# Order of the moving columns in the wide fp32r matmuls of a three-block network on one Trainium2 core

## What is computed

```python
def macaron_half_ffn(x, pre_g, post_g, w_gate, w_up, w_down):   # 1024 -> 2816 -> 1024
    h = rmsnorm(x, pre_g)
    h = (jax.nn.silu(h @ w_gate) * (h @ w_up)) @ w_down
    return x + 0.5 * rmsnorm(h, post_g)
...
def reference(x, ...):
    x = first_block(x, ...)    # ffn, sparse attention + short convolution, ffn; ffn, RWKV, ffn
    x = second_block(x, ...)   # ffn, SSD + attention, attention over a memory, ffn
    return third_block(x, ...) # 16 meta tokens ahead: ffn, gated linear attention, ffn; ffn, windowed attention, ffn
```

## Time and profile before

| | |
|---|---|
| three executions | 3,265.66, 3,267.18, 3,271.96 us; median 3,267.18 |
| the profiled execution | span 3,253.4 us from first to last instruction; the median lies 13.8 us above it |
| mean granted TensorE clock | 0.977 of full speed |
| PE, PEld (weight loads) | busy 96% and 92% of the span, 27,478 instructions each |
| DVE, ACT, POOL | busy 55%, 47%, 28% |
| HBM | 479 MB read, 148 GB/s over the span |

### The profile page before, as it was taken

The page is one execution under the profiler, slowest core; times in us unless marked ns, Lnnn a source line. Parts: engine busy times, 40 slices in busy tenths (PEclk is TensorE's granted clock), DMA queues, the critical chain, the costliest instruction groups (busy, mean ns, idle before and its releaser), DMA issues.

```text
span 3253.4 us, 64299 instructions
## 1 busy us (share of the span) xinstructions
PE 3111.1 (96%) x27478; PEld 2988.1 (92%) x27478; DVE 1803.0 (55%) x3040; ACT 1523.1 (47%) x2564; POOL 907.7 (28%) x481
## 2 busy tenths in 40 slices
PE   8999999999899999998999999999989999998999
PEld 8998899998688999998898889999979999997898
DVE  5456555647765645447567544454543546556554
ACT  5444454543422544437656444444333544544453
POOL 3321132331333232322221213222213332332232
PEclk9999999999999999999999999999989999998999
DMA  6542355564201555553343435535423454552354
GB/s 241 194 167 87 117 195 169 196 194 161 91 3 34 185 193 175 184 184 122 125 156 110 137 133 195 189 134 177 136 91 104 169 176 145 192 182 71 113 193 136
DMA packets 133388, 484.55 MB, mean 149 GB/s; under 512 B 14959, under 2 KB 17151, under 8 KB 132399
## 3 DMA queue, kind: packets, MB, share of 16 engines
q1 hardware_dynamic: 131120, 470.25, 43.1%
q0 software_dynamic: 1984, 10.19, 1.0%
HBM read 479.34 MB, written 1.05 MB: 148 GB/s over the span
## 4 chain that ended last, share of the span: by engine, by line
PE 82%; DVE 10%; ACT 5%; issue 2%; POOL 1%; DMA 0%; DVEq 0%; SPq 0%; ACTq 0%; POOLq 0%
PE ps L185 81%; DVE lo L162 2%; ACT hi L182 1%; ACT arena L182 1%; DVE tmp L170 1%; PE ps L193 1%; DVE sq L162 1%; DVE arena L170 1%; ACT L182 1%; DVE yT L170 1%; DVE arena L162 1%; POOL small L162 1%; POOL lo L162 0%; DVE small L179 0%; DVE xT L162 0%
## 5 line engine op out<-in xcount | busy, mean ns | idle before, releaser
L162 POOL TENSOR_TENSOR lo<-raw,hi 128x1024 fp32r<-128x1024 f32 x271 | 689.7, 2545 | 1683.3 <-ACT hi L182 1683.3
L182 ACT ACTIVATE hi<-raw 128x1024 fp32r<-128x1024 f32 x814 | 854.0, 1053 | 419.7 <-PE ps L185 312.2
L185 PE MATMUL ps<-hh,lo 128*128 128x256 f32 x3696 | 1019.5, 279 | 0.0
L162 DVE TENSOR_TENSOR lo<-raw,hi 128x1024 fp32r<-128x1024 f32 x543 | 703.7, 1299 | 513.6 <-ACT hi L182 493.4
L185 PE MATMUL ps<-hh,hi 128*128 128x256 f32 x3456 | 961.9, 281 | 24.3 <-ACT arena L182 8.8
L185 PE MATMUL ps<-hl,hi 128*128 128x256 f32 x3456 | 928.0, 279 | 1.2 <-DVE hl L162 1.2
L185 PEld LDWEIGHTS ps<-hh,lo 128*128 128x128 f32 x3696 | 702.6, 190 | 0.0
L185 PEld LDWEIGHTS ps<-hh,hi 128*128 128x128 f32 x3456 | 658.1, 190 | 32.8 <-ACT arena L182 12.2
L185 PEld LDWEIGHTS ps<-hl,hi 128*128 128x128 f32 x3456 | 641.6, 190 | 1.6 <-DVE hl L162 1.4
L185 PE MATMUL ps<-hfh,lo 128*128 128x256 f32 (+1 forms) x1760 | 489.5, 278 | 0.0
L185 PE MATMUL ps<-hfh,hi 128*128 128x256 f32 (+1 forms) x1520 | 422.7, 278 | 0.0
(11 more groups left out here) (385 smaller groups left out, 4716.6 us busy)
## 6 DMA issues: line engine op xcount, KB each, us to landing
raw<-in_l_ffn_w_gate SPq DMA_DIRECT2D x88, 512.0 KB, 3.3
raw<-in_l_ffn_w_up SPq DMA_DIRECT2D x88, 512.0 KB, 3.4
raw<-in_l_ffn_w_down SPq DMA_DIRECT2D x88, 512.0 KB, 3.6
raw<-in_g SPq DMA_DIRECT2D x88, 512.0 KB, 3.3
raw<-in_u SPq DMA_DIRECT2D x88, 512.0 KB, 3.3
raw<-in_d SPq DMA_DIRECT2D x88, 512.0 KB, 3.3
raw<-in_ffn_w_gate SPq DMA_DIRECT2D x44, 512.0 KB, 3.4
raw<-in_ffn_w_up SPq DMA_DIRECT2D x44, 512.0 KB, 3.5
```

Of the source, the lines that this page charges most:

```text
L162: return self.e.tensor_tensor(o, a, b, op)
L182: return self.e.activation(o, a, f, **kw)
L185: return self.e.matmul(o, a, b, start=first, stop=final, skip_group_check=loose)
```

## The change

The moving operand and the output of every matmul that goes through `mm3`, and of the two opening loops (`Ffn.firsts`, `Mixer.first`), get another order of columns where their number is a multiple of 256. The view `p (i a c) -> p a i c` with i = 2 and c = 4 takes columns 0 to 3 of the first half, 0 to 3 of the second half, 4 to 7 of the first, 4 to 7 of the second, and so on. Operand and output have the same order, so each result column is written to the place that it had. 272 columns are no multiple of 256 and stay as they were. The instructions, their order, waits and addresses of buffers are the same on all engines.

```diff
     def mm(self, o, a, b, first=True, final=True, loose=False):
         return self.e.matmul(o, a, b, start=first, stop=final, skip_group_check=loose)
 
+    def mw(self, o, a, b, first=True, final=True, loose=False):
+        return self.mm(halves(o), a, halves(b), first, final, loose)
+
     def mm3(self, o, a, b, first=True, final=True, loose=False):
-        self.mm(o, a[0], b[0], first, False, loose)
-        self.mm(o, a[0], b[1], False, False, loose)
-        return self.mm(o, a[1], b[0], False, final, loose)
+        self.mw(o, a[0], b[0], first, False, loose)
+        self.mw(o, a[0], b[1], False, False, loose)
+        return self.mw(o, a[1], b[0], False, final, loose)
...
+def halves(ap):
+
+
+    if ap.shape[-1] % 256:
+        return ap
+    return ap.rearrange("p (i a c) -> p a i c", i=2, c=4)
...
@@ Ffn.firsts
-                pe.mm(bank[:, 0:T], hi, K.X[T][0][:, k, 0:T], k == 0, False)
-                pe.mm(bank[:, 0:T], lo, K.X[T][0][:, k, 0:T], False, False)
+                pe.mw(bank[:, 0:T], hi, K.X[T][0][:, k, 0:T], k == 0, False)
+                pe.mw(bank[:, 0:T], lo, K.X[T][0][:, k, 0:T], False, False)
             pe.wait_ge(*self.entry.hl(k))
             for i, bank in enumerate(banks):
-                t = pe.mm(bank[:, 0:T], K.W.col(u + i, k)[0], K.X[T][1][:, k, 0:T], False, k == 7)
+                t = pe.mw(bank[:, 0:T], K.W.col(u + i, k)[0], K.X[T][1][:, k, 0:T], False, k == 7)
...
@@ Mixer.first
-                    pe.mm(bank[:, 0:T], w, src[0][:, k, 0:T], k == j == 0, False)
+                    pe.mw(bank[:, 0:T], w, src[0][:, k, 0:T], k == j == 0, False)
...
-                t = pe.mm(bank[:, 0:T], W.col(u + i, k)[0], src[1][:, k, 0:T], False, k == 7)
+                t = pe.mw(bank[:, 0:T], W.col(u + i, k)[0], src[1][:, k, 0:T], False, k == 7)
```

## The result

The changed kernel takes 3,455.3 us (median of 4 runs, 3,448.1 to 3,463.0) against 3,266.4 us for the kernel before beside it (3,256.4 to 3,272.0): a ratio of 1.058, 95% interval 1.054 to 1.062. It is slower by 5.8%, and lies above the end of my range.

A forecast was written before the change was run, and what follows sets the result against it. The prediction took TensorE's matmul spacing as the bound; savings of 27.8, 6.9 and 5.2 us, less a microsecond, gave 39 us off 3,267.2, so 3,228 us. The range was 3,188 to 3,340 us.

The forecast's parts named there:

- What bounds the kernel: Whole kernel: time is the number of wide matmuls times their spacing on TensorE, 113.3 ns, with TensorE 96% busy.
- What the spacing is made of: Wide fp32r matmuls: 6.6 ns over the array's time and the slower pace come from moving columns and next weights colliding.
- the second state: 256-column fp32r matmuls: same shapes and address remainders also run at 117.8 ns instead of 113.3; 1,098 intervals counted.
- the deeper gain: Rival for the 256-column matmuls: fp32r reaches the transposes' 110 ns or a little below, saving 66 us, 3,201 us; chance 0.18.
- The price of the new order: Split-order matmuls: shown by no row, so bounded; nearest taken as 111.5 ns, the pace of non-transposed 128-column fp32 rows.
- the sum: Changed 256- and 512-column matmuls: 27.8, 6.9 and 5.2 us saved, less a microsecond, gives 39 us.
- Half clock: About 300 matmuls at half clock gain nothing, taking a microsecond off the saving.
- No change: Rival for the whole kernel: time stays within 0.2% (6.5 us); chance 0.12.
- The slower rival: Every 256-column matmul pays the 117.8 ns pace, 73 us more, 3,340 us; chance 0.26, of it 0.10 beyond 3,340.

The follow-up runs named there:

- m3: Separate kernel without the network: blocks of 72 fp32r matmuls, one weight column repeated, many widths; 256 columns 113 and 118 ns in one piece, 126 split at 512 bytes.
- m1: Separate kernel without the network: blocks of 144 fp32r matmuls, varying split side, group size and weights; 114.1 ns in one piece, 127.2 with both split.
- m4: Separate kernel without the network: blocks of matmuls with weights cut to 4 and 16 columns, bf16 and plain fp32 added; one piece fp32r 114.7 ns, bf16 109.2.
- m2: Separate kernel without the network: blocks of 72 fp32r matmuls, halves further apart or groups at fixed steps; 127.6 ns at 512 bytes, 121.1 at 576, 134.5 stepping by 80.
- a2: Changed kernel with only the output in split order, moving operand read in one piece; 3,270.1 us, ratio 0.9995 to the kernel before.

## Why the prediction was wrong, point by point

- *What bounds the kernel* was right: TensorE's spacing, nothing else. The loss came through it, waits on converted weights stayed in single microseconds (4.7 and 3.7 us in total, for VectorE's and GpSimd's), and 272 columns and the other engines stayed as they were.
- *What the spacing is made of* is the step that failed. I put the 6.6 ns over the array's time, and the second state, down to the moving columns of one matmul and the weights of the next getting in each other's way. That was my estimate, and no run shows it. Rows 6 seemed to show that without this (2.51 - 0.28) / 20 = 111.5 ns, or the transposes' (1.04 - 0.27) / 7 = 110, are enough. But those rows are plain fp32, which takes (3.61 - 0.38) / 15 = 215.3 ns over 256 columns where fp32r takes 113.3; they show a read with slack, and the right comparison, a full-pace read without weights, was not in the trace of before. Measured, it is 113.3 ns with 4 weight columns: there was nothing to win but the second state's few us. I had seen that not one fp32r interval lay under 113 ns, and gave it too little weight against the deeper gain and none against the forecast.
- *The price of the new order*: taken 111.5, bounded above by 117.8, measured 126.7. No run shows the sum's 111.5 for 256 columns of fp32r, the least is 113.3. Nor does one show its 215.3 for 512 columns, which is plain fp32's spacing over 256: fp32r took 228 there before, 252 after, and 233 in one piece in the blocks. The 111.5 was no price of a read at all: fp32r with 128 or 192 moving columns takes 112.0 to 112.5 too (L35 and L39 of m3). The upper bound was the price of the second state, not of an unknown read pattern. The slowest row of that matmul, the half-clock one at 214, lay above what came, and I left it out of the range.
- *Half clock.* I took about 300 matmuls for it; the trace has 173. It is a microsecond of the sum and changes nothing.
- *No change* was nearer than my forecast as to the gain: one piece takes 114.1 ns with 128 weight columns (L34 of m1) and 114.7 with 4 (L32 of m4), so that less of the weights wins nothing. They aren't wholly without effect, though: their place moves the spacing of one piece by up to 6 ns (120.8 at L47 against 114.6 at L63 of m2).
- *The slower rival* had the sign, and the wrong price: the spacing is the same in gate, up and down products, but at 126.7 ns above 118, which I had set down as the mark that the jumps themselves cost. A time beyond 3,340 us by such a cost had a chance of 0.10 in the text, and came. Even this wasn't the whole: what a jump costs depends on where it leads and on the operand's type.
- *At the output* I gave the broken order no price of its own; it was worth nothing here (a2, ratio 0.9995).

## What to carry to other kernels

A fp32r moving operand at full clock should be read in one piece, or in runs of 256 bytes at least (free in the network, ratio 0.997; one kernel of blocks, m3, had 118.9 ns for such runs, the value of the second state). Of the finer orders tried here, those of bf16 and of plain fp32 in 16-byte groups were free (109.2 and 215.9 ns, as in one piece), and the one on the PSUM side (ratio 0.9995). Before a collision is put down as the reason of an excess, look for a row in which one of the two parties is missing while the other keeps its full pace; a row in which both run slower proves nothing. And ask of a row that gives a price whether something else sets it, as here, probably, the least time of a pair of weight load and matmul (112 ns). Where no row shows a new access pattern, the upper bound is the slowest row of that instruction, however far it lies.

## What the runs showed of the hardware that I had not expected

- fp32r doesn't reach the pace of bf16: 113.3 ns (or 117.8) for 256 columns and 233 for 512, where bf16 takes 109.2 and 215.8 with a weight load before each too.
- 256 columns are favoured: 272 take 123.3 to 126.7, 10 ns or more for 16 columns more. Fewer gain little: 128, 192 and 240 take 112.0, 112.5 and 113 with 128 weight columns.
- The distance between alternating 16-byte pieces of fp32r matters: 121 to 129 ns for 512 to 768 bytes, 134.5 for a step of 80 (m2).
- Writing PSUM in alternating groups of four fp32 columns costs nothing, also at 512 columns (33.85 us for a block of 144, L126 of m1, against 33.84 in one piece, L114).
